# Two prefetch slots for the modulation weights of the first recurrence, later sums, and one half of the output weights fetched during the last head

## The reference

```
ml = modulation(c[:, None, :], w_mod[l], b_mod[l])       # silu(c) @ w_mod[l] + b_mod[l], split in 6
mc = modulation(c_ctx[None, None, :], w_mod[l], b_mod[l])
hl = adaln(xl, g[0], ml[0], ml[1])                       # 512 rows; hc: 256 rows of context
yl, yc = mixer(hl, hc, w_in[l], w_out[l], ...)           # concat(recurrence 512, attention 256, fourier 256) @ w_out
xl = xl + ml[2] * rms_norm(yl, g[1])
xl = xl + ml[5] * rms_norm(swiglu(adaln(xl, g[2], ml[3], ml[4]), w_ffn_in[l], w_ffn_out[l]), g[3])
# inside mixer, per head (4 heads of 128), in both directions, chunkwise over 64 rows:
o, s = hgrn2_scan(q, v, z, lb, s0, reverse)              # gated recurrence
```

## Time and profile before

| | us |
|---|---|
| median of 3 runs | 3346.26 (3343.79 to 3348.17) |
| the profiled execution, its span | 3342.6 |
| PE busy | 3019.2 |
| DVE busy | 1578.4 |
| ACT busy | 988.3 |
| POOL busy | 320.9 |

### The profile page before, as it was taken

The page is one execution under the profiler, slowest core; times in us unless marked ns, Lnnn a source line. Parts: engine busy times, 40 slices in busy tenths (PEclk is TensorE's granted clock), DMA queues, the critical chain, the costliest instruction groups (busy, mean ns, idle before and its releaser), DMA issues.

```text
span 3342.6 us, 44104 instructions
## 1 busy us (share of the span) xinstructions
PE 3019.2 (90%) x18434; PEld 2410.6 (72%) x18434; DVE 1578.4 (47%) x3075; ACT 988.3 (30%) x1912; POOL 320.9 (10%) x594
## 2 busy tenths in 40 slices
PE   6988899999999998887699999999999787699998
PEld 4657688888976566777467888887656676478886
DVE  3122544445442255768663433425524656654444
ACT  2011423233341255334232221212225333232222
POOL 0000000000000000555300000000100234200001
PEclk9999899999999998998799999999999798799999
DMA  5433242222222110322503121121120011122322
GB/s 187 148 98 114 89 115 57 57 57 57 70 83 101 51 32 1 99 77 83 167 36 101 44 70 63 51 76 63 38 63 13 23 28 44 51 88 89 101 88 76
DMA packets 227235, 246.62 MB, mean 74 GB/s; under 512 B 5488, under 2 KB 192988, under 8 KB 225500
## 3 DMA queue, kind: packets, MB, share of 16 engines
q1 hardware_dynamic: 227036, 243.79, 22.7%
HBM read 234.34 MB, written 9.44 MB: 73 GB/s over the span
## 4 chain that ended last, share of the span: by engine, by line
PE 55%; DVE 9%; ACT 4%; issue 2%; DMA 1%; POOL 1%; SPq 0%; DVEq 0%; ACTq 0%; POOLq 0%
PE PS L1926 51%; PE PS L1930 2%; DVE AR L2654 1%; PE PS L2135 1%; ACT AR L174 1%; DVE AR L2645 1%; DVE AR L2890 1%; ACT L169 1%; DMA WR<-in_w_in 1%; POOL AR L2931 1%; DMA WR<-in_w_ffn_in 0%; DVE STAT L2826 0%; ACT WC L174 0%; ACT EX L174 0%; DVE EX L2877 0%
## 5 line engine op out<-in xcount | busy, mean ns | idle before, releaser
L1926 PE MATMUL PS<-HI,WC 128*128 128x512 f32 (+3 forms) x2144 | 571.5, 354 | 11.7 <-DVE WC L2871 7.6
L1926 PE MATMUL PS<-WR,HT 128*128 128x256 f32 (+2 forms) x2256 | 518.8, 388 | 16.8 <-ACT AR L174 6.3
L1926 PEld LDWEIGHTS PS<-WR,HT 128*128 128x128 f32 x2256 | 382.5, 199 | 129.3 <-issue 79.1
L1926 PEld LDWEIGHTS PS<-HI,WC 128*128 128x128 f32 x2144 | 381.8, 190 | 68.7 <-DVE WC L2871 9.3
L1926 PE MATMUL PS<-AR 128*64 128x64 f32 (+8 forms) x3756 | 329.4, 279 | 98.7 <-POOL AR L2931 34.5
L1926 PEld LDWEIGHTS PS<-AR 128*64 128x64 f32 (+5 forms) x3756 | 284.4, 182 | 150.6 <-issue 49.1
L1926 PE MATMUL PS<-LO,WC 128*128 128x512 f32 (+3 forms) x1072 | 379.0, 353 | 0.0
L174 ACT ACTIVATE AR<-PS 128x384 f32<-128x384 f32 (+4 forms) x383 | 164.7, 454 | 670.3 <-PE PS L1926 526.1
L1926 PE MATMUL PS<-HT,WR 128*128 128x256 f32 (+3 forms) x1136 | 347.4, 458 | 12.7 <-DMA WR<-in_w_in 6.9
L1926 PE MATMUL PS<-DW,DH 128*128 128x384 f32 (+1 forms) x1344 | 355.3, 346 | 0.9 <-DVE AR L2509 0.9
L2871 DVE TENSOR_TENSOR WC<-WR,WC 128x1024 fp32r<-128x1024 f32 x132 | 161.5, 1225 | 381.6 <-ACT WC L174 381.6
(11 more groups left out here) (287 smaller groups left out, 3427.5 us busy)
## 6 DMA issues: line engine op xcount, KB each, us to landing
WR<-in_w_ffn_in SPq DMA_DIRECT2D x44, 1024.0 KB, 7.0
WR<-in_w_in_b SPq DMA_DIRECT2D x51, 512.0 KB, 6.0
WR<-in_w_mod SPq DMA_DIRECT2D x12, 2048.0 KB, 8.0
WR<-in_w_mod SPq DMA_DIRECT2D x24, 1024.0 KB, 5.3
WR<-in_w_ffn_out SPq DMA_DIRECT2D x22, 1024.0 KB, 4.9
WR<-in_w_in SPq DMA_DIRECT2D x40, 512.0 KB, 4.1
WR<-in_w_out SPq DMA_DIRECT2D x8, 2048.0 KB, 9.1
WR<-in_w_in_a SPq DMA_DIRECT2D x8, 1024.0 KB, 5.3
```

Source lines behind the costliest of these rows:

```text
L1926: mm = lambda o, l, r, start, stop: e.o.matmul(o, l, r, start=start, stop=stop, skip_group_check=True)
```

## The change

Five edits. (1) A new slot `m` of 2048 columns and a buffer `MODB` of 256 columns lie at the end of the arena AR, which becomes larger since the program reserves less memory for dynamically issued DMAs (`dynamic_dma_scratch_size=1024`). (2) The chunks of w_mod[1] alternate between `q2` and `m`, and two are fetched ahead instead of one. (3) Products of the modulation stand six steps apart instead of seven, and four steps are put behind `mod_d`, so that a group still takes 32 steps. (4) The half c = 0 of w_out is fetched into slot 1 as soon as head 2 has ended, which is during head 3. (5) The half c = 1 is fetched after the loop, into slot 0; its place and that of c = 0 are thereby exchanged, at l = 0 and l = 1 alike.

```diff
--- before.py
+++ after.py
@@ -343,6 +343,9 @@
         P = Plan()
         wslots = {i: WR[:, 4096 * i:4096 * (i + 1)] for i in range(2)}
         wslots.update({f"q{i}": WR[:, 1024 * i:4096] for i in range(4)})
+        SPARE = ARN - 2304
+        wslots["m"] = AR[:, SPARE:SPARE + 2048]
+        MODB = AR[:, SPARE + 2048:SPARE + 2304]
         wuntil, wloads, wturn = {i: () for i in wslots}, Counter(), [0]
         quarters = [f"q{i}" for i in range(4)]
 
@@ -604,6 +607,9 @@
         def out_weights(wout):
             return [load(wout[:, 512 * c:512 * c + 512], 8, 512) for c in range(2)]
 
+        def out_half(wout, c, slot):
+            return load(wout[:, 512 * c:512 * c + 512], 8, 512, slot)
+
         def gates_applied(BRv, G):
 
             ns = [P.add("ga", BRv[:, i, :], G[:, i, :]) for i in range(4)]
@@ -622,6 +628,8 @@
                 if c < count:
                     chunks.append(load(A["w_mod_2"][l][:, width * c:width * c + width], 8, width, slot or slots[c]))
             chunk()
+            if width == 256:
+                chunk()
             yield
             for c0 in range(0, count, 4):
                 for q in range(4):
@@ -632,7 +640,7 @@
                     extra = more()
                     if extra:
                         chunk(extra)
-                    for _ in range(7 if width == 256 else 4):
+                    for _ in range(6 if width == 256 else 4):
                         yield
                 P.add("mod_h", halves, bank(b), n)
                 yield
@@ -644,6 +652,9 @@
                 yield
                 if width == 512:
                     yield
+                else:
+                    for _ in range(4):
+                        yield
 
 
 
@@ -1682,15 +1693,24 @@
                 if heads[3].gneed and spare:
                     wuntil["q0"] = (*wuntil["q0"], *wuntil["q1"])
                     return spare.pop()
-            mods = modulation(1, [XC[:, 1536:1664], WR[:, 7936:8192], AR[:, early.at:early.at + 128]], 7, ["q2"] * 24, width=256, more=freed) if both else iter(())
+            mods = modulation(1, [XC[:, 1536:1664], MODB, AR[:, early.at:early.at + 128]], 7, ["q2", "m"] * 12, width=256, more=freed) if both else iter(())
+            W = []
+
+            def first_half(steps, W=W, l=l, set_until=set_until, heads=heads):
+
+                for n, _ in enumerate(steps):
+                    if heads[2].ended and not W:
+                        wuntil[1] = set_until[2]
+                        W.append(out_half(A["w_out_2"][l], 0, 1))
+                    yield
             for h in range(4):
-                together(with_some(with_some(main(h), mods, MODS[h]), flow, FLOW[l]), preps[h], RATE[l][h], 1)
+                lead = main(h) if h < 3 else first_half(main(h))
+                together(with_some(with_some(lead, mods, MODS[h]), flow, FLOW[l]), preps[h], RATE[l][h], 1)
             carried_end()
             for _ in mods:
                 pass
             join_slot()
-            wuntil[1] = (*set_until[2], ("mod_t", P.count["mod_t"]))
-            W = out_weights(A["w_out_2"][l])
+            W.append(out_half(A["w_out_2"][l], 1, 0))
             fence()
             n = P.count["fence"]
             P.add("ld", "spill", X, XSP[:, 0:4096], n, (("spill", spilled[0]),))
@@ -3031,7 +3051,7 @@
     from concourse import mybir as _mybir
     from concourse.bass_utils import run_bass_kernel_spmd as _run
 
-    nc = _bacc.Bacc("TRN2", target_bir_lowering=False, num_devices=1)
+    nc = _bacc.Bacc("TRN2", target_bir_lowering=False, num_devices=1, dynamic_dma_scratch_size=1024)
     arrays, A = {}, {}
     for name in _INS:
         a = _np.ascontiguousarray(inputs[name])
```

## The result

The changed kernel takes 3356.9 us (median of 7 runs, 3354.4 to 3359.4), the kernel before in the same comparison 3347.0 (7 runs, 3343.8 to 3351.4). The ratio is 1.0026, with a 95% interval from 1.0015 to 1.0037: 9.9 us longer (5.0 to 12.4 by the interval), and more than the 0.2% named above. The forecast was 3355.5 us. The profiled spans are 3342.6 and 3353.1 us, 10.5 apart; the profiled execution of the changed kernel is the fastest of its seven.

What follows compares the result with a forecast made beforehand. Mostly PE-bound (3019.2 of 3342.6 us), so only gaps could be won; 13.5 + 0.7 + 0.5 + 3.6 - 3.4 - 5.7 = 9.2 us longer, 3346.26 + 9.2 = 3355.5 us, range 3345 to 3362.

Steps and rivals of the forecast that it cites:

- All of it is lost, 13.5 us: Both feed-forward starts: "up" waits for the w_out half multiplied last, 6.73 and 6.74 us later, 13.5 us lost.
- Crowding, 0.7: Both feed-forward starts: "down" issued right behind "up" slows that load, 0.35 us per layer, 0.7 us lost.
- The clock after the longer wait, 0.5: Behind PE's longer feed-forward waits: slow clock costs 0 to 3 us for both layers, 0.5 us taken.
- the rival value 0: Behind the feed-forward waits: a longer gap costs no more once the clock has fallen, sum lower by 0.5 us.
- The first output product, 5.7: Layer 0's first w_out product: no wait for w_out, faster first matmuls; 5.7 us gained, range 4.6 to 7.9.
- Chunks that move ahead, loss: Recurrence heads 0 to 2: earlier modulation chunks and sums delay outputs and gates; 3.6 us lost, from 3 gained to 6 lost.
- The end of the recurrence, -3.4: Layer 0's recurrence end: chunk waits go and sums move ahead of the output; 3.4 us gained, range 1.9 to 5.0.
- Even: Rival: PE's gaps absorb moved chunks and the clock stays high at the output product; 3348.5 us, chance 0.22.
- Faster: Rival: PE's order bounds the stage, each wait removed counts in full; 7.9 us less, 3338.4 us, chance 0.12.
- Crowded loads: Rival: loads disturb each other (3.0), clock takes 3.0, w_out half displaces a chunk; about 3363 us, chance 0.10.

Runs made afterwards that it cites:

- E1: Changed kernel with the feed-forward "up" weights staged in slot 1 and "down" in slot 0, both layers: 3344.7 us.
- E2: Kernel before with only the two w_out half edits, modulation timing as before: 3354.2 us, ratio 1.0021.
- E4: Kernel before with the w_out half edits plus "up" in slot 1 and "down" in slot 0, modulation as before: 3339.4 us.
- E10: E6 with DVE's modulation sums back at their old places, PE's chunks and transposes at the new ones: 3352.2 us.
- E7: Kernel before with only the smaller reserve for dynamically issued DMAs, every instruction unchanged: 3346.5 us.
- E6: Kernel before with only the new modulation places (products six steps apart, four steps behind each sum), one chunk slot: 3353.3 us.
- E3: Kernel before with only the modulation edits (two slots, six steps, four steps behind sums), both w_out halves after the loop: 3350.4 us.
- E11: Changed kernel with "up" in slot 1, "down" in slot 0, and DVE's modulation sums at their old places: 3343.1 us.
- E12: E6 with chunk products seven steps apart again; only ACT's copy, PE's transposes and DVE's sums stand earlier: 3347.9 us.

## Why the prediction was right, step by step

**"All of it is lost, 13.5 us": right.** PE's stands grew by 6.87 and 7.06 us, 13.9 with the crowding. E1 takes the growth away by the slot alone, and E2 brings it by the halves alone. This was the step that decided the sign, and it came from two rows of the kernel before: the issue of "down" told when the second half is done.

**Crowding, 0.7: at most 0.4.** E1 gives 0.2 us at each start, 10.70 against 10.51 and 10.78 against 10.56, where the kernel before and E1 differ by up to 0.1 among themselves. The prediction quoted the Trainium skill (DMA: Bandwidth & Descriptors, Queues, rings and completion order) for descriptors being consumed in ring order, and took from it that the first load loses nothing. Differences this small neither confirm nor contradict that.

**The clock after the longer wait, 0.5: should be 0.** E1 and the changed kernel have the same 0.70 after 3.80 and 10.73 us, and layer 1's rest is 0.4 us shorter, not longer. The Trainium skill (TensorE: Matmul & The Clock Gate, What's actually happening) calls the slow clock the default that activity releases, from which the prediction drew the rival value 0; the windows agree with that.

**The first output product, 5.7: slightly under-sized.** From the first transposes to EX it is 15.38 us instead of 21.75, 6.4 less, within the range of 4.6 to 7.9 (whose upper end should be 7.8, the sum of 4.6 and 3.2). The clock came back sooner, but it wasn't up all the time: twelve records took 6.13 us, against 8.39 before and 5.32 in E4. A further 1.6 us came one tile later, where the clock didn't fall behind a stand of 2.29 us as it had behind 2.31. That was in no term.

**"Chunks that move ahead, loss", 3.6: the mis-sized step.** Counted from the first output, the changed kernel is 5.7 us behind at head 2's last output, the ninth of twelve, which is where this term ends. (It is 3.6 behind at the tenth, 6.9 at the eleventh and 2.15 at the twelfth.) That is within the term's range of -3 to +6, near its end. The reason was partly wrong. I had DVE begin head 0's gates 7.2 us later and let that cost; they did begin 7.9 us later (39.58 us after the first output instead of 31.66), and E10 shows that it costs next to nothing. What costs is PE's chunk ahead of the output and the slow clock behind the transposes' wait: 3.7 us in head 0, where I had 1.8.

**The end of the recurrence, -3.4: right in sign, its size can't be told.** In head 3 the lag falls from 5.7 to 2.15 us, 3.55 less. Between its last two outputs alone 4.8 us come back, but the lag had grown there just before, since the transposes now stand ahead of the eleventh output. And 2.15 us come back between the ninth and the tenth, around the wait of 5.86 us for which I had counted nothing; whether that wait is the reason no run shows. The sum of the two terms doesn't hang on these places: from the first output to the fence (PE's first transposes, 1660.37 and 1662.47) the changed kernel loses 1.55 us, where I had 0.2. That difference is smaller than the scatter of single executions (E2, E7).

**The sum: in part luck.** Between spans 10.5 us were measured and 9.2 forecast. Of the 10.5, some 3 us (+0.55, +2.82 and -0.41 in the table) lie in stretches in which the change moves little, and E7 shows such differences with unchanged instructions. Without them 7.5 us are left, 1.7 below the forecast: 0.8 less at the feed-forward starts, 0.7 and 1.6 more gained at the output product and one tile later, 1.35 more lost in the recurrence. The interval of the medians, 5.0 to 12.4 us, holds 7.5 and 9.2 alike.

**The rivals.** *Even* rested on PE's gaps taking up the moved chunks; E6 (+6.6 us) excludes that. *Faster* rested on each wait taken off PE's queue counting in full; in E3 (+4.1 us) the 11.0 us of waits for sums and chunks are down to 0.6, and the kernel isn't faster. *Crowded loads* had 3.0 for crowding, and E1 leaves 0.4, and 3.0 for the clock, where the windows leave 0. Its 3363 us also needed 2.7 for a chunk pushed out, which I hadn't worked out; the chunks' waits are gone. The reserve costs nothing, as assumed (E7).

## What to carry to other kernels

When a load is moved to another buffer, look first at what is fetched into the old and the new one afterwards, and when each is let go: the buffer freed first should hold what is needed first. The repair here was to exchange the later loads too, and it turned 7.8 us of loss into 6.9 of gain. On an engine that works in order, put side work behind what another engine waits for, not ahead of it; a prefetch can be tried without moving any compute. And add up all waits of an engine, not only those that a change is to remove: here most of what went came back under other names.

## What the runs showed of the hardware

**The same short stand was free or dear.** In the second tile, stands of PE of 2.29 to 2.31 us were followed by a granted clock of 0.72 to 0.74 over 6 us in nine kernels and of 1.00 in five; that is 1.6 us. The eight kernels that had stood 3.8 to 4.6 us for w_out some 30 us earlier are among the nine. E11, which had not stood there, belongs to the nine as well, so that earlier stand isn't the condition, and what is stays open. In head 0 the picture is the same in every trace: six kernels (the changed one, E1, E3, E6, E10, E11) stand 2.14 to 2.16 us for the transposes and take 5.37 or 5.38 us for the 32 products behind them (granted clock 0.68 in the changed kernel and E10). E12 stands 1.01 us and takes 3.74, at 1.00.

**The length of a long stand didn't matter.** At layer 0's feed-forward start two kernels stood 10.73 and 10.84 us (the changed one and E2), and both had a granted clock of 0.70 over the next 10 us. The twelve others stood 3.71 to 4.02 us and had 0.69 to 0.86. At layer 1 it was 0.73 and 0.74 behind 10.80 and 10.63 us, and 0.72 to 0.74 behind 3.69 to 4.05. Why equal stands gave 0.69 in one execution and 0.86 in another stays open.
